# A two-layer hybrid trunk on one core: layer-norm sums on VectorE, five orders changed, and the last quarter of the first modulation cut in two

## The chip, the cores and the metric

The kernel runs on one core of a Trainium2 chip. Its engines are TensorE (PE; PEld is its weight load), VectorE (DVE), ScalarE (ACT), GpSimd (POOL) and SyncE (SP), which here only issues transfers. They run side by side and wait for each other through semaphores. The metric is the device time of one execution in microseconds (us); smaller is better.

## The reference, cut to what matters

Two layers act on x, 256 tokens of 2048 channels. All is float32.

```
cond = silu(c)
for layer in range(2):
    shift, scale, gate = split(cond @ w_ada[layer] + b_ada[layer])      # 2048 x 6144: the modulation
    h = rms_norm(x, norm_g) * (1 + scale) + shift
    qkv_a, z_a, ..., glu_in, z_b, q_c, k_c, v_c, z_c, ..., gate_raw = split(h @ w_in[layer])
    y_a = rms_norm(gated_delta_rule(...)) * silu(z_a)                   # branch a
    u   = causal_conv(a_half * sigmoid(b_half)) + conv_b_b
    y_b = silu(layer_norm(u)) * silu(z_b)                               # branch b: the layer norm over 1024 channels
    y_c = sparse_attention(...) * silu(z_c)                             # branch c
    merged = sum over a, b, c of sigmoid(gate_raw) * (y @ w_proj)
    x = x + gate * (merged @ w_out)
```

## The kernel before, in words

Activations lie channel by token: a tile `[128, KT, 256]` holds 16 blocks of 128 channels (`kt`), all 256 tokens in a row. Weights come in chunks of 256 rows by 512 columns (512 KB, two `kt`). A chunk passes four hands: SP loads it into one of four `raw` buffers (L377, after `w_split` says that the chunk four before it has been split), ACT rounds it into `wh` (L540, `rounds`, after PE has used the chunk four before it), POOL makes the rest `wl = raw - wh` (L519), and PE multiplies it (L908 to L910: three products for high and low halves). There are 672 chunks, 336 a layer. ACT's written order runs four chunks ahead of PE's. Every engine follows its own order written out by hand, so an instruction that waits holds up all that stands behind it on its engine. SP has one queue for all loads.

The stretches that the change touches, in order of time:

- **The first modulation** (layer 0). `cond @ w_ada` for shift and scale is done by DVE, in four quarters of 512 columns: `ada_part` (L1400 on) makes 16 multiply-adds of 128x1024 a quarter (512 columns of shift and of scale), from four `adaw` buffers that `ada_load` (L348) fills with 1 MB each, two `kt` at a time. The first three `kt` of the next quarter are done before `h_low` of this one. PE sums over partitions (`ada_sum(q)`, L988 to L991), DVE finishes the modulation (`quarter_mods`) and four blocks of h, ACT rounds them (`h_high`, L583), DVE makes the low half (`h_low`, L1477), and PE then runs its part of three pairs of PSUM banks over these four blocks (`part_gemm`, 144 products in six chunks). ACT's loop for quarter q is: round four chunks, `h_high(q)`, round two. After the fourth quarter a fourth pair follows over all 16 blocks.
- **The four turns of branch c** (`prep_turn`, L1737 on). While PE runs gate and projection products, DVE and PE work an inversion in levels; `between` is a hook of DVE behind levels 1 and 2. Turn 0 uses it.
- **The z groups.** 32 chunks, with the four steps of the scan between them. `ln_sum` (L1240) sums u over 1024 channels by eight products of `ones` with the eight blocks of `ub`; `ln_var` (L1247) does the same with the squares in `lnt`. ACT copies y_b to `yh` (L846) when DVE has it ready (`yb_ready`, L1912), between two stretches of `rounds`.
- **The turns of branches b and a.** DVE also accumulates the next modulations (`mod_unit`, 128x2048 from 1 MB `modw` buffers, two of them, `mod_load`, L389). A load of unit u waits until unit u-2 is done. `first` says from which `kt` the accumulator is in PSUM (banks 4 to 7) and not in SBUF (`acc`).
- **The output groups.** `w_out` in four groups of eight chunks, with the units of layer 1's scale between; `SCALE_AT` says behind which chunk (group, chunk) SP issues which unit's load, `UNIT_W` how many units DVE does before each group's result. At the layer's end PE sums the squares of x, ACT takes the root (`root_mean`, L545), and DVE and ACT build h of layer 1.

Of the kernel before, what the change touches and what calls it, by code (L numbers as in the profile page):

```python
# [24 lines left out]
P = 128  # L25
# [109 lines left out]
def trunk(nc, xt, cvec, rel_bias, w_ada, w_in, w_pa, w_pb, w_pc, w_out, b_gate, params, consts, hot, out):  # L135
    ctx = ExitStack()
    with ctx:
# [103 lines left out]
        lnt = sb("lnt", 122, [CT, T])  # L241

# [49 lines left out]
        def merged_ps(q):  # L292
# [31 lines left out]
        INV_Y = [11, 14, 17, 20, 23]  # L324

# [14 lines left out]
        def _(sp):  # L340
# [5 lines left out]
            def ada_load(n):  # L346

                q, j = n // 8, n % 8  # L348
                if n >= 4:
                    sp.wait_ge(sem("ada_used"), n - 3)  # L350
                for part in (SHIFT, SCALE):
                    col = part * D + q * GW
                    sp.dma_start(adaw[j % 4][:, :, part], wa[0, :, 2 * j:2 * j + 2, col:col + GW]
                                 ).then_inc(ada_landed[j % 4], 16)
# [14 lines left out]
            for layer in range(DEPTH):  # L369
# [154 lines left out]
        def _(act):  # L524
# [52 lines left out]
            for layer in range(DEPTH):  # L577
                L1 = layer + 1
                hc = layer * HCL
                def h_high(q):  # L580

                    act.wait_ge(sem("h_ready"), q + 1)
                    A.copy(ah[:, 4 * q:4 * q + 4], merged[:, 4 * q:4 * q + 4]).then_inc(sem("hh_ready"), 1)  # L583

                def shifted_high(n):

                    act.wait_ge(sem("h_ready"), 8 * layer - 4 + n + 1)
# [4 lines left out]
                if layer == 0:  # L592
                    for q in range(4):
# [3 lines left out]
                        hc += 6  # L597
                    rounds(hc, RING)
# [26 lines left out]
                for n, dst in enumerate((qk[:, 0:4], qk[:, 4:8], None, qi[:])):  # L625
# [7 lines left out]
                    if n == 0:  # L633
                        act.wait_ge(sem("hT_ready"), 8 * layer + 4)
# [208 lines left out]
                rounds(hc + 8, 2)  # L843
# [3 lines left out]
                rounds(hc + 10, 6, 2)  # L847
# [54 lines left out]
        def _(pe):  # L902
# [82 lines left out]
            def ada_sum(q):  # L985

                pe.wait_ge(sem("ada_summed"), q + 1)
                for part in (SHIFT, SCALE):  # L988
                    for j in range(4 * q, 4 * q + 4):
# [13 lines left out]
            for layer in range(DEPTH):  # L1003
# [10 lines left out]
                if layer == 0:  # L1014
# [3 lines left out]
                    for q in range(4):  # L1018
                        ada_sum(q)
                        pe.wait_ge(sem("hT_ready"), q + 1)  # L1020
                        for pair in range(3):
                            part_gemm(hc, pair, H, 4 * q, 4, G_IN)
                            hc += 2
# [3 lines left out]
                else:  # L1027
                    group(0, H, quarter=("hT_ready", 4 * layer, 1))
# [211 lines left out]
                def ln_sum():  # L1240
                    pe.wait_ge(sem("inv_u"), 6 * 4 * L1)
                    pe.wait_ge(sem("prep_wT"), 4 * L1 + 1)
                    for kt in range(CT):
                        mm = M.matmul(pb[3][:, 0:T], ones, ub[:, kt], start=kt == 0, stop=kt == CT - 1)
                    mm.then_inc(sem("ln_sum"), 1)

                def ln_var():  # L1247
                    pe.wait_ge(sem("ln_sq"), L1)
                    for kt in range(CT):
                        mm = M.matmul(pb[3][:, T:2 * T], ones, lnt[:, kt], start=kt == 0, stop=kt == CT - 1)  # L1250
                    mm.then_inc(sem("ln_var"), 1)
# [110 lines left out]
        def _(dve):  # L1362
# [29 lines left out]
            def normed_quarter(q):  # L1392

                V.tensor_tensor(merged[:, 4 * q:4 * q + 4], xs[:, 4 * q:4 * q + 4],
                                spread(rst[:], 1, [P, 4, T]), ALU.mult)

            def ada_part(q, k0, k1):

                wide, side = ps[:, 6:8, :], acc[:, :, q * GW:(q + 1) * GW]
                V.drain()  # L1400
                for kt in range(k0, k1):
                    j, m = kt // 2, kt % 2
                    if m == 0:
                        dve.wait_ge(ada_landed[j % 4], 32 * ((8 * q + j) // 4 + 1))
                    w = adaw[j % 4][:, m]
                    ahead = ADA_SIDE if q else 0
# [6 lines left out]
                    if m:  # L1413
# [624 lines left out]
```

## Time and profile before

| | us |
|---|---|
| median of 3 runs | 2340.78 (2339.74 to 2343.28) |
| the profiled execution | 2340.51 |
| its span, first to last instruction | 2338.7 |
| PE busy | 2255.2 (96%) |
| POOL busy | 1646.5 (70%) |
| DVE busy | 1141.1 (49%) |
| ACT busy | 955.9 (41%) |

A row of a timeline gives start and length of a run of like instructions, the engine, the line, what is written and read, and in brackets how long the engine had been idle and who ended that. A row of waits gives total, number of times and the longest. "The granted clock" is the share of full speed that TensorE had.

### The profile page before, as it was taken

To read this page: it belongs to the slowest core of one execution; us is meant where nothing else is said; L and a number is where in the kernel's file an instruction comes from. 1 tells how busy PE (TensorE), PEld (TensorE's weight loads), DVE (VectorE), ACT (ScalarE), POOL (GpSimd) and SP (SyncE) were. 2 spreads that over 40 slices of the span, in tenths; PEclk is the share of its full clock that TensorE was granted. 3 is DMA by queue.
4 is the path that set the end of the run, shared out by engine and by line. 5 is a ranking of instruction groups with operands and counts; after the bars stand their busy time and mean duration, and the time that the engine had idled before them with its cause. 6 is when DMAs were issued, how large, how long until landed. Compare 5 with 4: busy or idle time off the path is not lost.

```text
span 2338.7 us, 40293 instructions
## 1 busy us (share of the span) xinstructions
PE 2255.2 (96%) x16408; PEld 2040.3 (87%) x16408; DVE 1141.1 (49%) x1682; ACT 955.9 (41%) x1037; POOL 1646.5 (70%) x676
## 2 busy tenths in 40 slices
PE   5799999999999999999899999999999999999999
PEld 3789999987779988888899999998777899888899
DVE  5849883854443443443522894665544335421110
ACT  3234444472322544434234344437433244444442
POOL 1468778765554788987666886876655458888876
PEclk8789999999999999999999999999999999999999
DMA  9967545544442589897865664554444337976664
GB/s 370 386 210 225 164 142 177 161 148 124 129 137 92 200 310 332 296 329 284 323 208 181 195 213 142 168 166 145 138 134 134 113 118 279 343 233 190 204 207 154
DMA packets 228840, 479.65 MB, mean 205 GB/s; under 512 B 22080, under 2 KB 26304, under 8 KB 220128
## 3 DMA queue, kind: packets, MB, share of 16 engines
q1 hardware_dynamic: 227392, 475.50, 61.1%
q8 instruction: 99, 1.62, 0.3%
q10 hardware_dynamic: 1312, 2.23, 0.3%
q14 instruction: 37, 0.30, 0.0%
HBM read 471.25 MB, written 6.29 MB: 204 GB/s over the span
## 4 chain that ended last, share of the span: by engine, by line
POOL 48%; issue 35%; PE 16%; POOLq 1%; DVE 0%; ACT 0%; DVEq 0%; ACTq 0%
POOL wl L519 48%; PE ps L908 5%; PE ps L910 5%; PE ps L909 5%; POOLq L518 1%; PE ps L1331 0%; PE ps L997 0%; POOLq L514 0%; DVE xs L1985 0%; DVE ps L1709 0%; ACT gate L528 0%; POOLq L519 0%; DVEq L1367 0%; ACTq L770 0%; DVEq L1708 0%
## 5 line engine op out<-in xcount | busy, mean ns | idle before, releaser
L519 POOL TENSOR_TENSOR wl<-raw,wh 128x1024 fp32r<-128x1024 f32 x672 | 1646.3, 2460 | 679.2 <-ACT wh L540 677.8
L540 ACT CAST wh<-raw 128x1024 fp32r<-128x1024 f32 x672 | 702.8, 1049 | 1227.4 <-PE ps L910 1069.0
L908 PE MATMUL ps<-ah,wh 128*128 128x256 f32 x3008 | 873.8, 290 | 40.8 <-DVE al L1477 21.6
L909 PE MATMUL ps<-al,wh 128*128 128x256 f32 x3008 | 861.0, 286 | 0.0
L910 PE MATMUL ps<-ah,wl 128*128 128x256 f32 x3008 | 860.5, 286 | 0.0
L908 PEld LDWEIGHTS ps<-ah,wh 128*128 128x128 f32 x3008 | 588.0, 195 | 48.1 <-DVE al L1477 21.9
L909 PEld LDWEIGHTS ps<-al,wh 128*128 128x128 f32 x3008 | 587.8, 195 | 4.5 <-issue 4.1
L910 PEld LDWEIGHTS ps<-ah,wl 128*128 128x128 f32 x3008 | 587.4, 195 | 0.0
L908 PE MATMUL ps<-wh,ah 128*128 128x512 f32 (+1 forms) x832 | 325.7, 391 | 0.0
L910 PE MATMUL ps<-wh,al 128*128 128x512 f32 (+1 forms) x832 | 318.7, 383 | 0.0
L909 PE MATMUL ps<-wl,ah 128*128 128x512 f32 (+1 forms) x832 | 318.5, 383 | 0.0
L1543 DVE SCALAR_TENSOR_TENSOR ps<-upad,par,ps 128x256 f32<-128x256 f32 x480 | 199.7, 484 | 9.3 <-issue 0.4
L908 PEld LDWEIGHTS ps<-wh,ah 128*128 128x128 f32 x832 | 157.3, 189 | 31.2
L910 PEld LDWEIGHTS ps<-wh,al 128*128 128x128 f32 x832 | 157.0, 189 | 31.0
L909 PEld LDWEIGHTS ps<-wl,ah 128*128 128x128 f32 x832 | 157.4, 189 | 28.3
L1430 DVE SCALAR_TENSOR_TENSOR ps<-modw,cond,ps 128x2048 f32<-128x2048 f32 x50 | 117.8, 2356 | 111.0 <-DMA modw<-w_ada 107.4
L908 PE MATMUL ps<-wh,yh 128*128 128x512 f32 x384 | 155.5, 405 | 0.0
L909 PE MATMUL ps<-wl,yh 128*128 128x512 f32 x384 | 150.0, 391 | 0.0
L910 PE MATMUL ps<-wh,yl 128*128 128x512 f32 x384 | 149.8, 390 | 0.0
L1709 DVE TENSOR_TENSOR ps<-ps,gbias 128x1024 f32<-128x1024 f32 x24 | 29.5, 1230 | 138.5 <-PE ps L910 138.5
L908 PEld LDWEIGHTS ps<-wh,yh 128*128 128x128 f32 x384 | 72.0, 188 | 16.1 <-POOL wl L519 0.2
L910 PEld LDWEIGHTS ps<-wh,yl 128*128 128x128 f32 x384 | 72.1, 188 | 15.5
(259 smaller groups left out, 1810.9 us busy)
## 6 DMA issues: line engine op xcount, KB each, us to landing
raw<-w_in SPq DMA_DIRECT2D x512, 512.0 KB, 3.5
modw<-w_ada SPq DMA_DIRECT2D x64, 1024.0 KB, 7.6
adaw<-w_ada SPq DMA_DIRECT2D x64, 512.0 KB, 9.6
raw<-w_out SPq DMA_DIRECT2D x64, 512.0 KB, 5.0
raw<-w_pc SPq DMA_DIRECT2D x32, 512.0 KB, 3.6
raw<-w_pb SPq DMA_DIRECT2D x32, 512.0 KB, 5.7
raw<-w_pa SPq DMA_DIRECT2D x32, 512.0 KB, 4.9
gbias<-b_gate SPq DMA_DIRECT2D x24, 256.0 KB, 4.3
```

Source lines behind the costliest of these rows:

```text
L518: pool.wait_ge(sem("w_rounded"), i * SPLITS + (n + 1))
L519: nc.gpsimd.tensor_tensor(wl[:, s], raw[:, s], wh[:, s].bitcast(F32), ALU.subtract).then_inc(sem("w_split"), 1)
L540: A.copy(wh[:, s], raw[:, s]).then_inc(sem("w_rounded"), 1)
L908: M.matmul(o, lh, rh, start=start, stop=False, skip_group_check=True)
L909: M.matmul(o, lh, rr, start=False, stop=False, skip_group_check=True)
L910: return M.matmul(o, ll, rh, start=False, stop=last, skip_group_check=True)
L1430: unit = V.scalar_tensor_tensor(o, w, cond[:, kt:kt + 1], wide if first < kt <= last else side, ALU.mult, ALU.add)
L1543: V.scalar_tensor_tensor(o, upad[:, ct, back:back + T], w, o, ALU.mult, ALU.add)
L1709: V.tensor_tensor(ps[:, 0:2, :], ps[:, 0:2, :], spread(gbias[:], 1, [P, TT, GW]), ALU.add).then_inc(sem("gate_sum"), 1)
```

## The change

1. *Last quarter in two.* `PIECES` makes five pieces of the first modulation: three of 512 columns, two of 256. A load for a half piece brings four `kt` of 256 columns (1 MB as before). DVE does 16 multiply-adds of 128x512 for each half; of the last piece only `kt` 0 is done ahead. PE's `ada_sum(3)` stands between pair 1 and pair 2 of the third piece. SP's chunks of the last quarter come in the order of the halves. ACT's loop keeps its order, with `h_high(4)` behind it.
2. *Layer-norm sums.* DVE adds up the eight blocks (`tensor_reduce` over a view with 256 elements from one value to the next), for the sum in the hook of turn 2, for the squares behind `scan_v(2)`; PE makes one product of each.
3. *yh.* Three more chunks are rounded ahead of the copy to `yh`.
4. *Output groups.* `UNIT_S` 2 to 3, unit 2 of the last turn moves ahead of `merged_low(0)`; groups 0 to 3 do 2, 5, 5, 0 units in place of 4, 4, 4, 0; loads are placed anew.
5. *Root.* A one-column Sqrt on ACT behind the last three chunks, ahead of the squares.

```diff
-        UNIT_A, UNIT_W, UNIT_S = 4, 4, 2
+        UNIT_A, UNIT_S = 4, 3
+        UNIT_W = (UNIT_A, 6, 11, KT)
-        SCALE_AT = {(0, 3): 4, (0, 5): 5, (0, 6): 6, (0, 7): 7, (1, 1): 8, (1, 3): 9, (1, 5): 10, (1, 7): 11,
-                    (2, 1): 12, (2, 3): 13, (2, 5): 14, (2, 7): 15}
+        SCALE_AT = {(0, 4): 4, (0, 7): 5, (1, 1): 6, (1, 3): 7, (1, 4): 8, (1, 6): 9, (1, 7): 10,
+                    (2, 1): 11, (2, 3): 12, (2, 4): 13, (2, 6): 14, (2, 7): 15}
...
+        PIECES = ((0, GW), (GW, GW), (2 * GW, GW), (3 * GW, GW // 2), (3 * GW + GW // 2, GW // 2))
+        FIRST = len(PIECES)
...
-                    chunks = [(col, j) for q in range(4) for col in (first, second, first + GW)
-                              for j in range(2 * q, 2 * q + 2)]
+                    chunks = [(col, j) for q in range(3) for col in cols for j in range(2 * q, 2 * q + 2)]
+                    chunks += [(col, j) for j in (6, 7) for col in cols]
...
                         rounds(hc, RING, hc % RING)
                         h_high(q)
                         rounds(hc + RING, 2, (hc + RING) % RING)
                         hc += 6
+                    h_high(4)
...
-                rounds(hc + 8, 2)
+                rounds(hc + 8, 5)
                 act.wait_ge(sem("yb_ready"), L1)
                 act.wait_ge(sem("w_used"), proj_end)
                 A.copy(yh[:], ub[:]).then_inc(sem("yh_ready"), 1)
-                rounds(hc + 10, 6, 2)
+                rounds(hc + 13, 3, 1)
...
                     rounds(hc, 3)
+                    A.activation(craw[:, 0:1], epsb[:, 0:1], ACT.Sqrt)
...
-                    for q in range(4):
-                        ada_sum(q)
+                    for q in range(FIRST):
+                        if q != 3:
+                            ada_sum(q)
                         pe.wait_ge(sem("hT_ready"), q + 1)
...
                         for pair in range(3):
-                            part_gemm(hc, pair, H, 4 * q, 4, G_IN)
-                            hc += 2
+                            if q == 2 and pair == 2:
+                                ada_sum(3)
+                            part_gemm(hc, pair, H, tiles.start, n, G_IN)
+                            hc += n // HK
...
-                    for kt in range(CT):
-                        mm = M.matmul(pb[3][:, 0:T], ones, ub[:, kt], start=kt == 0, stop=kt == CT - 1)
-                    mm.then_inc(sem("ln_sum"), 1)
+                    pe.wait_ge(sem("ln_tiles"), L1)
+                    M.matmul(pb[3][:, 0:T], ones, lss[:, 0], start=True, stop=True).then_inc(sem("ln_sum"), 1)
...
+                        ahead = ADA_SIDE if q < FIRST - 2 else 0
...
-                        ada_part(q, ADA_SIDE + 1 if q else 10, KT)
+                        ada_part(q, 10 if q == 0 else ADA_SIDE + 1 if q < FIRST - 1 else 1, KT)
-                        if q < 3:
-                            ada_part(q + 1, 0, ADA_SIDE)
+                        if q < FIRST - 1:
+                            ada_part(q + 1, 0, ahead)
                         quarter_mods(q)
...
-                        if q < 3:
-                            ada_part(q + 1, ADA_SIDE, ADA_SIDE + 1)
+                        if q < FIRST - 1:
+                            ada_part(q + 1, ahead, ahead + 1)
                         h_low(q)
...
+                def ln_tiles(n):
+
+                    if n == 0:
+                        V.tensor_reduce(lss[:, 0], ub[:].rearrange("p c t -> p t c"), AX.X, ALU.add
+                                        ).then_inc(sem("ln_tiles"), 1)
...
-                    prep_turn(i, split_yc if i == 0 else None)
+                    prep_turn(i, split_yc if i == 0 else ln_tiles if i == 2 else None)
...
                 scan_v(2)
+                V.drain()
+                V.tensor_reduce(lss[:, 1], lnt[:].rearrange("p c t -> p t c"), AX.X, ALU.add
+                                ).then_inc(sem("ln_sq"), 1)
                 z_silu(2, 0, zs[1])
...
+                units(2, 3)
                 for q in range(3):
                     merged_low(q)
                 merge(3, hc, 12 * layer + 8, False)
-                units(2, 4)
+                units(3, 4)
                 merged_low(3)
...
-                            for kt in range(UNIT_A + UNIT_W * j, UNIT_A + UNIT_W * (j + 1)):
+                            for kt in range(UNIT_W[j], UNIT_W[j + 1]):
```

## Rows read from the trace of the kernel before

**Rows 1.** The page's first line.
```profile
span 2338.7 us, 40293 instructions
```
**Rows 2.** Waits of PE, whole span: total us, times, longest.
```profile
PE ps L908 <- DVE al L1477: 21.6, 4, 6.4
PE ps L990 <- DVEq L1415: 17.4, 4, 13.4
PE ps L908 <- POOL wl L519: 12.9, 6, 3.8
PE ps L908 <- issue: 6.3, 1, 6.3
```
**Rows 3.** Timeline of PE, the third and fourth quarter.
```profile
115.31 0.58 PE L908 MATMUL ps<-ah,wh 128*128 128x256 f32 x1 [6.37 <-DVE al L1477]
...
136.72 2.13 PE L990 MATMUL ps<-con,acc 128*128 128x1 f32 x16 [1.27 <-DVEq L1415]
143.23 0.58 PE L908 MATMUL ps<-ah,wh 128*128 128x256 f32 x1 [4.39 <-DVE al L1477]
```
**Rows 4.** Timeline of DVE, the fourth quarter.
```profile
116.47 9.53 DVE L1411 SCALAR_TENSOR_TENSOR ps<-adaw,cond,ps 128x1024 f32<-128x1024 f32 x7
...
135.34 1.28 DVE L1411 SCALAR_TENSOR_TENSOR acc<-adaw,cond,ps 128x1024 f32<-128x1024 f32 x1
...
139.46 1.38 DVE L1501 TENSOR_SCALAR merged<-merged,gsc,mods 128x256 f32<-128x256 f32 x4
141.95 1.23 DVE L1477 TENSOR_TENSOR al<-merged,ah 128x1024 fp32r<-128x1024 f32 x1 [1.11 <-ACT ah L583]
```
**Rows 5.** Timeline of ACT, the end of the fourth quarter.
```profile
135.54 1.05 ACT L540 CAST wh<-raw 128x1024 fp32r<-128x1024 f32 x1 [1.83 <-PE ps L910]
140.87 1.04 ACT L583 CAST ah<-merged 128x1024 fp32r<-128x1024 f32 x1 [4.29 <-DVE merged L1501]
```
**Rows 6.** DVE's instructions by line and form: busy us, mean ns.
```profile
L1759 DVE TENSOR_TENSOR vb<-ps,hbeta 128x512 f32<-128x512 f32 x8 | 5.5, 693 | 0.2
```
**Rows 7.** Windows of 5 us: PE, PEld, DVE, ACT, POOL busy, granted clock, DMA share, GB/s.
```profile
825.00:830.00 5.00, 4.66 (x22) 4.66 (x23) 0.53 (x1) 0.00 (x0) 4.96 (x4) 0.50 0.75 269
...
1145.00:1150.00 5.00, 5.00 (x44) 5.00 (x43) 3.06 (x2) 2.09 (x2) 4.57 (x3) 1.00 1.04 405
```
**Rows 8.** Timeline of PE, the first layer-norm sum.
```profile
703.29 3.62 PE L1244 MATMUL ps<-ub,con 128*128 128x256 f32 x16
```
**Rows 9.** DVE's instructions by line and form: a reduction.
```profile
L1634 DVE TENSOR_REDUCE mx<-probs 128x8 f32<-128x2048 f32 x2 | 4.6, 2286 | 0.1
```
**Rows 10.** Timeline of DVE in turn 2 and behind the third step of the scan.
```profile
677.46 0.42 DVE L1789 TENSOR_TENSOR xm<-ps,con 128x256 f32<-128x256 f32 x1 [3.27 <-PE ps L1192]
...
743.08 1.22 DVE L1700 SCALAR_TENSOR_TENSOR zs<-zt,ps 128x1024 f32<-128x1024 f32 x1 [5.16 <-ACT zt L528]
```
**Rows 11.** Timeline of PE, the waits behind the copy to yh.
```profile
825.34 0.58 PE L908 MATMUL ps<-ah,wh 128*128 128x256 f32 x1 [3.43 <-POOL wl L519]
...
1964.42 0.57 PE L908 MATMUL ps<-ah,wh 128*128 128x256 f32 x1 [2.33 <-POOL wl L519]
```
**Rows 12.** Timeline of ACT, the first copy to yh.
```profile
818.85 1.90 ACT L846 CAST yh<-ub 128x2048 fp32r<-128x2048 f32 x1 [7.31 <-DVE ub L1912]
```
**Rows 13.** Waits of PE from 1100 to 1200 us.
```profile
PE ps L908 <- POOL wl L519: 6.8, 3, 3.8
```
**Rows 14.** Timeline of SP's queue, the first output group.
```profile
1087.14 11.59 SPq L377 DMA_DIRECT2D raw<-w_out  x4
1115.55 0.34 SPq L389 DMA_DIRECT2D modw<-w_ada  x1
```
**Rows 15.** Timeline of DVE, unit 2 of the scale.
```profile
1113.01 2.51 DVE L1430 SCALAR_TENSOR_TENSOR ps<-modw,cond,acc 128x2048 f32<-128x2048 f32 x1 [0.29 <-issue]
```
**Rows 16.** Timeline of ACT, the root at the layer's end.
```profile
1226.44 1.28 ACT L545 ACT_TABLE_LOAD   x1
```
**Rows 17.** Timeline of PE, the last sum of squares.
```profile
1224.76 1.99 PE L970 MATMUL ps<-merged,con 128*128 128x256 f32 x8 [1.63 <-ACT merged L895]
```

More of the change, by code:

```diff
@@ L988, in ada_sum @@
                 for part in (SHIFT, SCALE):
-                    for j in range(4 * q, 4 * q + 4):
+                    for j in range(piece_tiles(q).start, piece_tiles(q).stop):
                         mm = M.matmul(pb[2][:, part * KT + j:part * KT + j + 1], acc[:, part, j * P:(j + 1) * P],
@@ L1027, in _ @@
                 else:
-                    group(0, H, quarter=("hT_ready", 4 * layer, 1))
+                    group(0, H, quarter=("hT_ready", FIRST * layer, 1))
                     group(1, H)
@@ L1392, in normed_quarter @@
             def normed_quarter(q):
-                V.tensor_tensor(merged[:, 4 * q:4 * q + 4], xs[:, 4 * q:4 * q + 4],
-                                spread(rst[:], 1, [P, 4, T]), ALU.mult)
+                tiles = piece_tiles(q)
+                V.tensor_tensor(merged[:, tiles], xs[:, tiles],
+                                spread(rst[:], 1, [P, tiles.stop - tiles.start, T]), ALU.mult)
             def ada_part(q, k0, k1):
-                wide, side = ps[:, 6:8, :], acc[:, :, q * GW:(q + 1) * GW]
+                (first, per), (at, width) = piece_loads(q), PIECES[q]
+                wide, side = ps[:, 6:8, at % GW:at % GW + width], acc[:, :, at:at + width]
                 V.drain()
                 for kt in range(k0, k1):
-                    j, m = kt // 2, kt % 2
+                    j, m = first + kt // per, kt % per
                     if m == 0:
-                        dve.wait_ge(ada_landed[j % 4], 32 * ((8 * q + j) // 4 + 1))
-                    w = adaw[j % 4][:, m]
-                    ahead = ADA_SIDE if q else 0
+                        dve.wait_ge(ada_landed[j % 4], 32 * (j // 4 + 1))
+                    w = piece_weights(adaw[j % 4], q)[:, m]
+                    ahead = ADA_SIDE if 0 < q < 4 else 0
                     o = wide if ahead <= kt < KT - 1 else side
@@ L1453, in quarter_mods @@
             def quarter_mods(q):
[L1455 removed]
+                part = piece_tiles(q)
+                k0, n = part.start, part.stop - part.start
                 dve.wait_ge(sem("ada_turned"), q + 1)
[L1457 to L1460 removed]
+                for side in (SHIFT, SCALE):
+                    at = side * KT + k0
+                    last = V.tensor_tensor(mods[:, at:at + n], pb[2][:, at:at + n], p_(0, "b_ada", at, n), ALU.add)
+                if q == FIRST - 1:
                     last.then_inc(sem("mods_ready"), 1)
                 V.drain()
[L1463 to L1464 removed]
+                V.scalar_tensor_tensor(gsc[:, part], mods[:, KT + k0:KT + k0 + n], 1.0,
+                                       p_(0, "norm_g", k0, n), ALU.add, ALU.mult)
                 V.drain()
@@ L1487, in _ @@
                 if layer == 0:
-                    for q in range(4):
+                    for q in range(FIRST):
+                        ahead = ADA_SIDE if q < FIRST - 2 else 0
                         if q == 0:
@@ L1496, in _ @@
                             dve.wait_ge(sem("con_landed"), 16)
-                        if q < 3:
-                            ada_part(q + 1, 0, ADA_SIDE)
+                        if q < FIRST - 1:
+                            ada_part(q + 1, 0, ahead)
                         quarter_mods(q)
-                        for kt in range(4 * q, 4 * q + 4):
+                        for kt in range(piece_tiles(q).start, piece_tiles(q).stop):
                             m = V.tensor_scalar(merged[:, kt], merged[:, kt], gsc[:, kt:kt + 1], mods[:, kt:kt + 1],
```

51 lines of the change are left out of this document (30 added, 21 removed).

## The prediction

> **What bounds the kernel now.** I read the page first. The span is 2338.7 us [rows 1] and the execution took 2340.51, 1.81 outside the span; the median of the runs is 2340.78, so the sum below, made against 2340.51, stands for the median within 0.3. PE is busy in 96% of the span, POOL in 70%, DVE in 49%: PE sets the time, and a change is worth what it takes from PE's own work or from PE's waits. So the second view is the list of PE's waits [rows 2]. Four groups matter: 21.6 us before the products that need h of a quarter, 17.4 before the sums of the first modulation, 12.9 in six waits for POOL's halves, and one of 6.3 at the layer's end (named "issue"; the root's chain lies in it). The third view is each engine's timeline around them. A wait costs more than its length: behind the one of 3.43 [rows 11] the granted clock is 0.50, TensorE's lower level of 1.2 GHz, and a window of 5 us holds 22 products, where another at 1.00 holds 44 [rows 7]. About 26 products of 0.21 us run there instead of at 0.12, so I add 2.6 us to a wait of this length.
>
> **First modulation: +2.9.** Take it in the order of time. The units of the fourth quarter done ahead become half as wide. A unit of 1024 takes 1.36 from start to start (9.53 for 7) [rows 4]; a two-input instruction of 512 from PSUM takes 0.69 [rows 6], a multiply-add is 0.07 longer and the gap behind it 0.07, so 0.83. Two such units stand ahead of the third quarter's h, so PE starts that (third) quarter at 113.9 and not at 115.31 [rows 3]: -1.4. Its 144 products end 20.1 later as before (136.72 less 1.27 idle is 135.45 [rows 3]), and the sum for the first half, half of the 2.13 [rows 3], now stands between them: 135.1. DVE has its half long done (13 units of 0.83 behind h_low and the norm: 125.4), but waits for that sum until 129.3, since PE takes it only behind pair 1; nothing else stands ahead of DVE's wait, because no unit of the last half is done ahead of it. Then it makes two blocks of h by 130.7 and one unit of the last half.
>
> Here is the step that I think decides. ACT's order was not changed: it rounds four chunks and only then does h_high(3). The fourth of them, row 135.54, waits for PE's use of the last chunk of the third quarter [rows 5]. Before, that cost nothing, because h came at 140.87 [rows 5]; now h is ready at 130.7 and ACT sits in front of the rounding until 135.1. Rounding 1.05, h_high on half the elements 0.6, h_low half of 1.23 [rows 4]: PE gets the first half's h at 137.4, so it stands 2.3 us, and DVE stands too, from 131.6 to 136.8. Only then come the norm of two blocks (0.7) and 15 units of 0.83, 12.5: the last sum is ready at 150.6, where the whole quarter was ready at 136.6 before (135.34 + 1.28 [rows 4]). The loads do not bind: their last unit before ran at 135.34, and now none is read before 138. PE's 72 products for the first half (8.6) end at 146. Behind 150.6 come the sum (1.1), the modulation (0.6), two blocks (half of 1.38), h_high 0.6 and h_low 0.65 [rows 4, 5]: 154.6. The 72 products left take 8.6, and 2 more at the lower clock: 165.2. Before, PE started at 143.23 [rows 3] and 144 products took 17.3 and 2.3: 162.8. With 0.5 for the clock behind the earlier start: **+2.9**. Bounds: if DVE's short units run at 0.69 and the clock rises early, 2 us less and 1 more for it, so 0; if a short unit costs as much as half a long one plus a whole 0.3 of overhead (0.98), 15 of them add 2.3, and late loads of 1 KB rows 1 more: +6.
>
> **Layer-norm sums: -12.1.** A sum of eight products is 16 records in 3.62 with the tail of the last, 3.45 from start to start [rows 8]; two products' records of 16 stay, so 14 x 0.216 = 3.0 go. There are four (two a layer): -12.1. PE is full there, so the whole is path, if DVE's reductions are covered. A reduction of 2048 contiguous values takes 2.29 [rows 9]. In turn 2 DVE idles 3.27 before the row 677.46 [rows 10]; the reduction stands in that gap, and PE reads the next `xm` 1.5 later, so 4.2 are free. Behind scan_v(2) DVE idles 5.16 before 743.08 [rows 10]. `ln_var` is asked for some 11 us behind scan_v(2). At 2.29 both are hidden. No row shows the strided view: bounds 2.29 and four times that, 9.2; I take 2.3 to 4.2, cost 0. At 9.2 the first delays PE by 5 a layer.
>
> The Trainium skill (Advanced Engine Details and Errata, section Memory Cachelines) speaks against this: reads that hit a different 16-byte line each time pay a penalty, and here each value is 1 KB from the next. It names no size. By the page the reduction is longer than row 9's; by the sum nothing is owed until it passes 4.2. It is a rival below.
>
> **yh: -6.0 and -3.9.** ACT waits 7.31 for y_b [rows 12] and copies for 1.90, and the chunk behind reaches PE late: 3.43 and 2.33 of wait [rows 11]. With three more chunks rounded first, these are ready in time (PE uses one in 2.88, and they are asked for from 822 on); the copy runs from 820.1 and not 818.85, between two roundings. Behind it, chunk 13 of the row is rounded 1 late, with 6 to spare; DVE's low half of y is 1.3 later, and PE asks for it over 20 us later. SP's next unit loads wait for units behind that low half: a mod load moves to 827 from 830, so it keeps ahead of PE, which gains 6. Layer 0: 3.43 + 2.6 = -6.0. Layer 1: 2.33 and a shorter stretch of low clock, 1.6: -3.9. Bounds: nothing lost, or half given back to loads: -5 to -10.
>
> **Output groups: -9.0.** SP stands between 1098.7 (1087.14 + 11.59) and 1115.55 [rows 14], because the load behind chunk (0,3) waits for unit 2, which DVE does at 1113.01 [rows 15], behind a merge. The `w_out` chunks queued behind it come late, and PE waits 6.8 in three waits [rows 13], the first of 3.8 [rows 2], with the 2.6 of clock behind it. With unit 2 done before merged_low(0), at 1096 to 1100, in ACT's shadow, and the load one chunk later, chunk (0,4) is issued at 1103.4. The waits go: -9.4. What is late next: SP stands at (1,4) for unit 6, which DVE does behind group 0's result (PE ends that group at 1133.6, result 1.7, unit 2.4: 1137.9). The unit's load and chunk (1,5) behind it then land by 1144.2, rounding 1.05 and POOL 2.4 end at 1147.6, and PE comes to this chunk at 1148.0. Groups 1 and 2 hold 5 loads of 1.05 MB and 8 chunks of 0.52, 9.4 MB: at the 405 GB/s of a full window [rows 7] 23.3 us against PE's 23.0, so it stays that close, chunk after chunk, through both; I take 0.4 of wait. **-9.0**, bounds -4 (each of groups 1 and 2 loses 2.5) and -10.
>
> **Root: -0.9.** ACT loads its table from 1226.44 for 1.28 [rows 16] while PE's last sum of squares ends at 1226.75 (1224.76 + 1.99) [rows 17]. The load now falls in ACT's idle time before the squares. The root can start at 1226.8 and not 1227.7: -0.9, within the 6.3 wait [rows 2]. Bounds 0 and -1.3.
>
> **Sum.** +2.9 - 12.1 - 6.0 - 3.9 - 9.0 - 0.9 = -29.0. 2340.5 - 29.0 = 2311.5, which stands for the median.
>
> **Rivals.**
> - *The half pays.* ACT and DVE pass the first half sooner than I think, and the start of the layer gains: the term is 0 or below (-3 at the end). For it: DVE idles 5 us in this stretch by my sum. Against: row 135.54. Time 2306 to 2308.5. Chance 0.15.
> - *The loads bind the output groups.* SP's waits at (1,4) and (2,4) come late enough to empty the queue, and half of the 9.0 is given back. Time 2316. For it: 23.3 against 23.0. Chance 0.15.
> - *The strided reduction is slow.* At 9.2 us it delays the inversion in turn 2 by 5 a layer: 2321.5. Chance 0.07. This is the rule of the page above.
> - *Slower than before.* The same mechanism further on: in turn 2, PE waits for every us beyond 4.2; behind scan_v(2) for every us beyond about 11. The gain of 29.0 is used up when a layer loses 14.5, that is at a reduction of about 15 us (10.8 + 4), 7.3 ns a value against 1.1 in row 9's. Then the time is 2341 and above that slower. Nothing in the rows is so slow. Chance 0.02.
> - *The change does not do what it says.* The waits behind yh stay, because POOL and not ACT holds the chunks (its halves take 2.4, PE's chunk 2.88). Then 10 are missing: 2321. Chance 0.04.
>
> **Numbers.** The forecast has 0.57, with its own range 2308 to 2315. To reach 8 in 10 and to take in the bounds (start 0 to +6, output -4 to -10, yh -5 to -10) the range goes from 2304 to 2319. A change of 0.2% (4.7 us) is about what can be told here. Faster: 0.96; within: 0.02; slower: 0.02.
>
> **What would show it.** PE's wait for the first half's h at about 135 to 137.5, ended by ACT's order (h_high(3) behind the rounding of chunk 21), and its first product of the last half near 154.6. Lines of the layer-norm sums with 2 records each and no wait. No wait for POOL behind yh; at most 1 us of it between 1100 and 1200. One table load less in front of the root. DVE's reductions at 2.3 to 4.2. The forecast is wrong if the start of the fourth pair is not 2 to 4 later than before, if a reduction passes 4.2, or if waits for POOL in the output groups pass 2 us.

## The result, and the profile after

The changed kernel takes 2320.89 us (2320.60 to 2321.02, 4 runs) where the kernel before took 2340.26 beside it (2338.14 to 2343.28, 4 runs): ratio 0.9916, 95% interval 0.9902 to 0.9930. It is 19.4 us faster; 29.0 were forecast. The profiled execution took 2320.99 with a span of 2319.2, against 2340.51 and 2338.7 [rows 1], so the two traces differ by 19.5 and can be laid side by side. One execution of a kernel below, the one with the layer-norm sums alone, took 2804.78 at a granted clock of 0.73 and is left out of its median.

First, where PE waits. The view of PE's waits in the changed kernel (engine, what and line waited for, total us, times, longest), which answers to [rows 2]:

```profile
PE ps L931 <- DVE al L1506: 29.1, 5, 8.1
PE ps L1013 <- DVEq L1442: 17.6, 2, 15.7
PE ps L931 <- POOL wl L539: 5.3, 10, 0.8
PE ps L931 <- issue: 5.3, 1, 5.3
```

POOL's waits fell from 12.9 in six to 5.3, but in ten: the long ones went and small ones came. The waits for h rose from 21.6 in four to 29.1 in five.

Second, in which stretch the time went. All 672 weight chunks come in the same order on PE in both kernels, except the last six of the first modulation, so I took the time at which PE ends each chunk, and compared the length of the stretches between such times. Layers and their parts are those of the text on the kernel before; differences to the kernel before, in us; chunks that are not listed moved by 0.0:

| stretch (chunks) | forecast | measured |
|---|---|---|
| first modulation (to 23) | +2.9 | +6.4 |
| from there to the z groups (to 175) | 0 | -1.9 |
| layer-norm sums, layers 0 and 1 (176-187, 512-523) | -12.1 | -6.05, -6.05 |
| chunks behind the copy to yh (206-207, 542-543) | -6.0, -3.9 | -6.3, -4.1 |
| the turns behind them (208-255, 544-591) | 0 | +3.5, +1.1 |
| output groups 0 and early 1 (304-316) | -9.4 | -10.1 |
| the rest of the output groups (317-335) | +0.4 | +3.4 |
| root and first chunks of layer 1 (336-339) | -0.9 | -0.4 |
| all others (256-303, 340-511, 592-end) | 0 | -1.6, +0.9, +1.6 |
| sum | -29.0 | -19.5 |

*The start.* PE, then ACT, then DVE in the changed kernel (start and length in us, engine, line, what, count, idle before and who ended it); the PE rows answer to [rows 3], the others to [rows 4, 5]:

```profile
141.33 0.58 PE L931 MATMUL ps<-ah,wh 128*128 128x256 f32 x1 [5.93 <-DVE al L1506]
154.47 1.05 PE L1013 MATMUL ps<-con,acc 128*128 128x1 f32 x8 [1.98 <-DVEq L1442]
158.29 0.58 PE L931 MATMUL ps<-ah,wh 128*128 128x256 f32 x1 [2.77 <-DVE al L1506]
...
137.27 1.04 ACT L560 CAST wh<-raw 128x1024 fp32r<-128x1024 f32 x1 [3.30 <-DMA raw<-w_in]
138.22 0.61 ACT L604 CAST ah<-merged 128x512 fp32r<-128x512 f32 x1
...
130.13 2.72 DVE L1531 TENSOR_SCALAR merged<-merged,gsc,mods 128x256 f32<-128x256 f32 x2
...
138.87 2.41 DVE L1506 TENSOR_TENSOR al<-merged,ah 128x512 fp32r<-128x512 f32 x1 [5.16 <-ACT ah L604]
...
141.96 11.59 DVE L1438 SCALAR_TENSOR_TENSOR ps<-adaw,cond,ps 128x512 f32<-128x512 f32 x14
```

The order is the one forecast: h's two blocks are ready at 132.85 (130.13 + 2.72), yet ACT rounds them at 138.22, right behind a rounding of weights. That rounding waited for its load and not, as I wrote, for PE alone: it began at 137.27, where I had it begin at 135.1. PE got the first half's h at 141.33 (forecast 137.4) and the last half's at 158.29 (forecast 154.6). The 14 units of 0.83 are as forecast (11.59 for 14).

Why that load was late is in SP's queue and in one window of each trace, the first two rows from the changed kernel, the last from the kernel before (columns of the windows as in [rows 7]):

```profile
127.66 25.95 SPq L396 DMA_DIRECT2D raw<-w_in  x7
106.00:137.00 31.00, 22.29 (x170) 21.80 (x169) 21.06 (x32) 7.34 (x7) 15.29 (x7) 0.83 1.09 361
```
```profile
106.00:136.00 30.00, 22.65 (x160) 22.36 (x160) 24.65 (x26) 6.96 (x8) 14.22 (x6) 0.77 1.04 380
```

SP issued the load at 127.66, about as before (127.58), and it landed at 137.25, where before it landed at 135.22. The transfer engines are full in both kernels (shares 1.09 and 1.04), but they move 361 GB/s and not 380: two thirds of the bytes now come in rows of 1 KB (the half pieces), and such a row takes 51 ns where one of 2 KB takes 89. The load was close to binding before, too: it landed 0.32 ahead of the rounding at 135.54 [rows 5].

POOL's rows of the same stretch say why a pair of DVE instructions that takes 0.73 at 156.12 took 2.72, and one that takes 0.69 at 157.54 took 2.41:

```profile
129.98 2.40 POOL L539 TENSOR_TENSOR wl<-raw,wh 128x1024 fp32r<-128x1024 f32 x1 [0.49 <-ACT wh L560]
134.05 2.38 POOL L539 TENSOR_TENSOR wl<-raw,wh 128x1024 fp32r<-128x1024 f32 x1 [1.67 <-ACT wh L560]
138.39 2.34 POOL L539 TENSOR_TENSOR wl<-raw,wh 128x1024 fp32r<-128x1024 f32 x1 [1.97 <-ACT wh L560]
```

Each of the two DVE rows begins inside a POOL half and ends some 0.5 behind it: 132.85 against 132.38, 141.28 against 140.73. DVE seems to have stood until POOL was nearly through. The Trainium skill (SBUF — State Buffer, section Who interferes with whom) has this as an exclusive lock between DVE and GpSimd, taken by DVE's instructions with two SBUF inputs and by some with one; both rows fit it.

*Layer-norm sums.* DVE's reductions by line and form (busy us, mean ns); contiguous values took 2286 [rows 9]. Behind them PE's first sum:

```profile
L1923 DVE TENSOR_REDUCE lss<-lnt 128x256 f32<-128x2048 f32 x2 | 7.8, 3882 | 0.2
L1856 DVE TENSOR_REDUCE lss<-ub 128x256 f32<-128x2048 f32 x2 | 7.7, 3825 | 0.0
...
707.79 0.60 PE L1272 MATMUL ps<-lss,con 128*128 128x256 f32 x2
```

The strided view costs 1.7 times the contiguous one. This agrees with the rule on 16-byte lines in the Trainium skill (Advanced Engine Details and Errata, section Memory Cachelines), which names no size; here it is 3.9 us and not 9, under the 4.2 from which it would cost. PE's part fell from 3.62 [rows 8] to 0.60 with 2 records.

*yh.* DVE and then POOL in the changed kernel, behind the first copy to yh:

```profile
813.01 4.33 DVE L1951 SCALAR_TENSOR_TENSOR ub<-ub,zs 128x2048 f32<-128x2048 f32 x1
820.46 3.67 DVE L1953 TENSOR_TENSOR yl<-ub,yh 128x2048 fp32r<-128x2048 f32 x1 [3.12 <-ACT yh L868]
...
810.74 27.15 POOL L539 TENSOR_TENSOR wl<-raw,wh 128x1024 fp32r<-128x1024 f32 x8
```

POOL makes eight halves without a pause and takes 3.39 each, over PE's 2.88 a chunk. Then PE waits 0.33, 0.68 and 0.78 for it at 826, 836 and 853, and again at 957. The two long waits of [rows 11] are gone.

*Output groups.* SP's queue, then windows of 10 us in the changed kernel (PE, PEld, DVE, ACT, POOL busy, granted clock, DMA share, GB/s):

```profile
1122.73 0.37 SPq L396 DMA_DIRECT2D raw<-w_out  x1
1131.99 0.34 SPq L408 DMA_DIRECT2D modw<-w_ada  x1
...
1130.00:1140.00 10.00, 10.00 (x86) 10.00 (x85) 6.68 (x3) 2.10 (x2) 3.90 (x3) 1.00 0.70 240
1140.00:1150.00 10.00, 9.36 (x76) 8.95 (x75) 4.67 (x2) 3.05 (x3) 7.06 (x3) 1.00 1.03 411
```

The first output group no longer waits. SP's stand for unit 6 is there as forecast, and it lasts 9 us (1123.1 to 1131.99). The load ahead of it landed at 1129.76, so the queue was empty for over 2 us (DMA share 0.00 from 1130 to 1132, 0.70 until 1140), and then full at 411 GB/s while PE runs short.

*Root.* The table load is out of the chain (ACT loads it at 1208.83, PE's sums of squares start at 1212.18), and PE's wait "issue" is 5.30 where it was 6.26 (the 6.3 of [rows 2]). It is 5.30 or 5.31 in every kernel below with the early Sqrt, and 6.25 in the three without.

### The profile page after: what moved, and what is told of

Read it like the earlier page. It is cut to its first block, busy times and chain, and to the rows that moved or that the text cites. A ratio compares the mean times of both kernels' runs of the same rounds, so it can differ in the third digit from the quotient of the medians.

```text
span 2319.2 us, 40232 instructions
## 1 busy us (share of the span) xinstructions
PE 2236.6 (96%) x16352; PEld 2022.0 (87%) x16352; DVE 1174.9 (51%) x1707; ACT 956.2 (41%) x1039; POOL 1655.5 (71%) x676
## 4 chain that ended last, share of the span: by engine, by line
POOL 48%; issue 35%; PE 15%; POOLq 1%; DMA 0%; DVE 0%; ACT 0%; DVEq 0%; ACTq 0%
POOL wl L539 48%; PE ps L931 5%; PE ps L933 5%; PE ps L932 5%; POOLq L538 1%; PE ps L1356 0%; DMA raw<-w_in 0%; PE ps L1020 0%; POOLq L534 0%; DVE xs L2025 0%; DVE ps L1739 0%; ACT wh L560 0%; ACT gate L548 0%; POOLq L539 0%; DVEq L1392 0%
## 5 line engine op out<-in xcount | busy, mean ns | idle before, releaser
L931 PE MATMUL ps<-ah,wh 128*128 128x256 f32 x3008 | 871.9, 290 | 36.6 <-DVE al L1506 29.1
```

The source lines that it names most:

```text
L931: M.matmul(o, lh, rh, start=start, stop=False, skip_group_check=True)
```

## The experiments

Each kernel ran with the kernel before on the same chip. Single executions there mostly lie within 4 us of their median, a few 7 or 8 off, the kernel before too (2335.66 to 2349.85 in all), and move with the granted clock (0.981 to 0.974). So differences of 2 or 3 us between two kernels are read from the stretches and not from the medians. The differences to the kernel before, in the stretches of the table above:

| kernel | start | to 175 | sums, both | yh, both | turns, both | out 304-316 | out 317-335 |
|---|---|---|---|---|---|---|---|
| changed, first profile | 6.4 | -1.9 | -12.1 | -10.4 | 3.5, 1.1 | -10.1 | 3.4 |
| changed, again | 6.6 | -3.4 | -12.1 | -10.4 | 1.6, 1.2 | -10.1 | 3.9 |
| no halves | 0.1 | 0.0 | -12.1 | -10.4 | 2.6, 1.3 | -10.1 | 3.8 |
| h rounded earlier | 1.0 | -1.8 | -12.1 | -10.4 | 0.6, 1.7 | -10.1 | 3.6 |
| groups 4, 4, 4 | 6.1 | -1.9 | -12.1 | -10.4 | 1.1, 1.2 | -10.1 | -1.6 |
| one SBUF input | 6.5 | -3.3 | -12.1 | -10.4 | -0.1, 0.0 | -10.1 | 3.6 |
| narrow gate loads | 6.9 | -3.3 | -12.1 | -10.4 | 1.4, 1.7 | -10.1 | 4.9 |
| three repairs | -1.3 | -3.3 | -12.1 | -10.4 | 2.3, 1.1 | -10.1 | 0.0 |
| no halves, groups 4, 4, 4 | 0.7 | 0.1 | -12.1 | -10.4 | 1.7, 1.5 | -10.1 | -1.6 |
| sums alone | 0.1 | 0.1 | -12.1 | -0.5 | 1.0, 0.0 | 2.8 | -1.6 |
| yh alone | 0.3 | 0.0 | 0.0 | -10.4 | 1.1, 0.7 | -0.1 | 0.0 |
| output alone | 0.9 | 0.0 | 0.0 | -3.1 | -0.1, 0.3 | -10.1 | 4.5 |

**The changed kernel with the first modulation as before (no halves).** All other parts of the change stay.

```
-        PIECES = ((0, GW), (GW, GW), (2 * GW, GW), (3 * GW, GW // 2), (3 * GW + GW // 2, GW // 2))
...
+                    for q in range(4):
+                        ada_sum(q)
```

> The changed kernel with the first modulation as before (four quarters); layer-norm sums, yh, output groups and root stay as changed. Theory (the halves cost what the two traces show: the fourth pair of the first stage starts 6.4 us later, because ACT's order holds h_high(3) behind the rounding of chunk 21 and DVE then has 15 short units left): 2320.9 - 6.4 = 2314.5, and PE's first product of the last quarter starts near 143 again. Rival (the halves gain and what is missing lies elsewhere): above 2321. Rival (they cost only the 2.9 us that I forecast): 2318.

Measured: 2315.99 (2308.66 to 2317.33), ratio 0.9883 (0.9864 to 0.9902). The start falls back to +0.1. The halves cost 6.3 in the start. Of that, 1.8 to 3.4 comes back before chunk 175 in every kernel with halves, and nothing in those without: the low clock near 290 is shorter or absent there (last section).

**h of the first half rounded earlier.** ACT rounds two chunks and not four before it.

```
-                        rounds(hc, RING, hc % RING)
+                        early = 2 if q == 3 else RING
+                        rounds(hc, early, hc % RING)
                         h_high(q)
-                        rounds(hc + RING, 2, (hc + RING) % RING)
+                        rounds(hc + early, 6 - early, (hc + early) % RING)
```

> The changed kernel with one order changed on ACT: in the last quarter it rounds two chunks, then does h_high(3), then rounds four (before: four, h_high(3), two). Theory (ACT's order is the cause): h_high(3) runs near 133 instead of 138.2, PE starts the first half near 135.5 instead of 141.3, DVE starts its 15 units 5 us earlier, and the time falls by 4 to 5.5 us to about 2316. Rival (the short units and the loads, not ACT's order, are the cost): PE's wait moves to the second half and the time stays within 1 us of 2320.9.

Measured: 2315.48 (2311.8 to 2320.2), ratio 0.9894 (0.9878 to 0.9910). Its PE, ACT and DVE rows:

```profile
148.54 1.87 PE L1014 MATMUL ps<-con,acc 128*128 128x1 f32 x8 [3.61 <-DVEq L1443]
153.18 0.58 PE L932 MATMUL ps<-ah,wh 128*128 128x256 f32 x1 [2.77 <-DVE al L1507]
...
133.78 0.62 ACT L604 CAST ah<-merged 128x512 fp32r<-128x512 f32 x1 [2.99 <-DVE merged L1532]
...
134.67 0.69 DVE L1507 TENSOR_TENSOR al<-merged,ah 128x512 fp32r<-128x512 f32 x1
```

ACT now takes h the moment DVE has it (133.78), DVE's low half finds POOL idle and takes 0.69, and PE has no wait of the first half left. The last half's h comes at 153.18 and not at 158.29, and the start falls by 5.4, to +1.0. So ACT's order is the cause of that much, as the prediction's "step that decides" says.

**Output units in groups of 4, 4, 4, 4.** Each group does four units, so the unit that waits for a group's result comes later in the queue.

```
-        UNIT_W = (UNIT_A, 6, 11, KT)
+        UNIT_W = (UNIT_A, 8, 12, KT)
-        SCALE_AT = {(0, 4): 4, (0, 7): 5, (1, 1): 6, (1, 3): 7, (1, 4): 8, (1, 6): 9, (1, 7): 10,
-                    (2, 1): 11, (2, 3): 12, (2, 4): 13, (2, 6): 14, (2, 7): 15}
+        SCALE_AT = {(0, 4): 4, (0, 7): 5, (1, 1): 6, (1, 2): 7, (1, 4): 8, (1, 6): 9, (1, 7): 10,
+                    (2, 1): 11, (2, 2): 12, (2, 4): 13, (2, 5): 14, (2, 7): 15}
```

> The changed kernel with groups 0 to 2 of the output doing 4, 4, 4 units (in place of 2, 5, 5) and the loads placed to match. Theory (SP stands until 1132 for unit 6, which waits for group 0's result, so the queue runs dry and the loads then bind: 3.4 us given back): unit 6 runs near 1123, the load behind (1,4) is issued near 1125 instead of 1132, and 2.5 to 3.4 us come back: about 2318. Rival (9.4 MB a group against 23.0 us of PE bind by themselves, wherever the loads stand): within 1 us of 2320.9.

Measured: 2317.46 (2313.09 to 2318.77), ratio 0.9899 (0.9884 to 0.9913). SP's queue and the two windows in this kernel:

```profile
1123.88 0.34 SPq L408 DMA_DIRECT2D modw<-w_ada  x1
1124.31 3.23 SPq L396 DMA_DIRECT2D raw<-w_out  x2
...
1130.00:1140.00 10.00, 10.00 (x86) 10.00 (x85) 4.75 (x3) 3.58 (x4) 9.08 (x5) 1.00 1.02 388
1140.00:1150.00 10.00, 10.00 (x85) 10.00 (x84) 5.22 (x4) 3.15 (x3) 8.20 (x4) 1.00 1.02 391
```

The load behind chunk 3 of the group goes out at 1123.88 and not at 1131.99, the transfer engines are full from 1130 on, and no wait of PE for POOL stands between 1100 and 1200. The stretch falls from +3.4 to -1.6. Of these 5.0, the queue is 3.4: the other 1.6 is clock, a low stretch behind the sums of the scale that stands at 1200 in the kernel before and at 1188 in the changed one and is missing here. The same bytes pass: an empty queue is what cost, not the rate.

**The changed kernel again,** on the chip of the next three.

> The changed kernel once more, as it stands, so that the kernels beside it have it on their own chip. No theory differs on it: 2321 by its first runs, and of the stretches of its matmul row the layer-norm ones and the output ones as before; turns of branch b of layer 0 give back between 0.6 (as with the third rounding moved) and 3.5 us, if the amount depends on which low-clock windows and loads an execution gets.

Measured: 2321.95 (2321.09 to 2328.88), ratio 0.9915 (0.9896 to 0.9934), as at first. The turns of layer 0 give back 1.6 here and gave back 3.5 in the first profile: the amount is a matter of the execution. PE's waits for POOL there are 0.85 in place of 2.37, and DVE's four large two-input instructions beside them took 12.8 in place of 15.4.

**One SBUF input.** The four DVE instructions of 128x2048 with two SBUF inputs around the copy to yh become instructions of one input. Left out: the products with the norm's gate and with zs, and the true low half of y_b.

```
-                V.scalar_tensor_tensor(ub[:], ub[:], 0.25, zs[1][:], ALU.mult, ALU.mult).then_inc(sem("yb_ready"), 1)
+                V.tensor_scalar(ub[:], ub[:], 0.25, None, ALU.mult).then_inc(sem("yb_ready"), 1)
...
-                V.tensor_tensor(yl[:], ub[:], yh[:].bitcast(F32), ALU.subtract).then_inc(sem("y_split"), 1)
+                V.tensor_scalar(yl[:], ub[:], 0.001, None, ALU.mult).then_inc(sem("y_split"), 1)
```

> Leaves out the product with the norm's gate, the product with zs and the true low half of y_b and y_a: the four VectorE operations of two SBUF inputs over 128x2048 that stand between the gating units become operations of one SBUF input. Theory (GpSimd's weight halves are slow beside VectorE operations of two SBUF inputs, and that is what gives back 3.5 of the 6.3 us in layer 0): the GpSimd halves there stay near 2.4 us instead of 4.4, VectorE's four operations fall from 15.4 to under 10 us together, and the turns of branch b of layer 0 give back 0.5 us or less (-3), layer 1's 0.3 (-0.8): 2317. Rival (GpSimd runs back to back there since its order was caught up by TensorE, whatever VectorE does, or the loads come late by themselves): give-back stays at 2.5 or more, within 1 us of the changed kernel.

Measured: 2315.10 (2312.62 to 2315.35), ratio 0.9878 (0.9859 to 0.9897); 6.9 below the changed kernel beside it, more than the 4 expected. POOL in this kernel, the same stretch:

```profile
811.91 13.93 POOL L539 TENSOR_TENSOR wl<-raw,wh 128x1024 fp32r<-128x1024 f32 x5
826.04 2.41 POOL L539 TENSOR_TENSOR wl<-raw,wh 128x1024 fp32r<-128x1024 f32 x1 [0.19 <-ACT wh L560]
828.73 7.84 POOL L539 TENSOR_TENSOR wl<-raw,wh 128x1024 fp32r<-128x1024 f32 x3 [0.29 <-ACT wh L560]
```

Nine halves take 24.2, 2.69 each, where eight took 27.15, and POOL waits for ACT again instead of being behind. DVE's four instructions took 8.9 together. Nothing is given back in either layer (-0.1, 0.0), where the changed kernel beside it gave back 1.6 and 1.2. That is 2.9; another 3.1 is clock, in stretches no edit touches (256-303 and 592 on). This bears out the theory and excludes the rival that POOL falls behind whatever DVE does. The edit took an input away and made the instructions shorter at once, so it can't tell these two apart.

**Narrow gate loads.** Units 2 to 15 of layer 0's gate bring an eighth of their columns, so their results are not the gate's. An earlier form, which narrowed units 0 and 1 too, gave no result; in it I had still held the loads for the cause.

```
+                    wide = D // 8 if l == 0 and part == GATING and kt > 1 else D
```

> Loads an eighth of the columns for units 2 to 15 of layer 0's gate projection (the rest of each tile is stale data; the multiply-adds have the same sizes), so that some 12 MB less are loaded in and after the turns of layer 0's input projection. Theory (the weight halves on GpSimd are late, not the loads): the give-back in the turns of branch b falls by at most 1.5 us of the 3.5, since only what hangs on late loads goes. Rival (the transfer queues are what the gained time runs into): give-back falls to 0.5 or less, 3 us faster than the changed kernel, and the DMA share of the window falls below 0.8 with no wait of GpSimd on raw left.

Measured: 2321.95 (2319.07 to 2326.06), ratio 0.9909 (0.9891 to 0.9927): nothing. Windows of 814 to 834 in the changed kernel, and then in this one:

```profile
814.00:834.00 20.00, 19.67 (x135) 18.19 (x134) 16.44 (x7) 9.09 (x9) 19.96 (x7) 1.00 0.81 299
```
```profile
814.00:834.00 20.00, 19.76 (x130) 17.77 (x128) 14.18 (x7) 9.90 (x9) 19.96 (x7) 1.00 0.68 203
```

The DMA share falls from 0.81 to 0.68 and POOL stays at 19.96 of 20; the turns give back 1.4. In layer 0, the loads are not what the gained time ran into.

**Three repairs in one.** h rounded earlier, groups of 4, 4, 4, 4, and three of the last half's units done in `acc` ahead of its turn.

```
-                    ahead = ADA_SIDE if 0 < q < 4 else 0
+                    ahead = 0 if q == 0 else ADA_SIDE if q < 4 else 3
...
-                        ada_part(q, 10 if q == 0 else ADA_SIDE + 1 if q < FIRST - 1 else 1, KT)
+                        ada_part(q, 10 if q == 0 else ADA_SIDE + 1 if q < FIRST - 1 else 4, KT)
...
+                        if q == 3:
+                            ahead = 3
```

> The changed kernel with three edits: the rounding of h's first half ahead of all but two weight roundings, three units of the last half's multiply-adds ahead of its turn (acc in SBUF), and the output units in groups of 4, 4, 4, 4. Theory: ACT's order costs 5.3 us at the start, the halves' units after the first half 2.5 us more, the gap of the output groups 5.0 us: start +6.4 becomes -1 to -2, output +3.4 becomes -1.6; 2321 - 12.8 = 2308, and 2306 to 2311 by the clock. Rival (the start's loss is the low clock that follows any stop of that length, and it comes back at another place; the loads of the output matrix are what binds at 1140): 2313 or more.

Measured: 2307.00 (2304.64 to 2311.85), ratio 0.9848 (0.9827 to 0.9869), the best of all and as expected (2308). PE's rows and one of DVE's:

```profile
135.94 0.38 PE L932 MATMUL ps<-ah,wh 128*128 128x256 f32 x1 [1.06 <-DVE al L1507]
146.57 1.05 PE L1014 MATMUL ps<-con,acc 128*128 128x1 f32 x8 [1.75 <-DVEq L1443]
150.39 0.58 PE L932 MATMUL ps<-ah,wh 128*128 128x256 f32 x1 [2.77 <-DVE al L1507]
...
129.32 3.56 DVE L1439 SCALAR_TENSOR_TENSOR acc<-adaw,cond,acc 128x512 f32<-128x512 f32 x2
```

The last half's h is at 150.39, 2.8 before that of the second experiment: three units of 0.83 are 2.5. In `acc`, in SBUF, two units take 3.56 beside POOL's half and not 1.6, but in time that was idle. The output's rest came to 0.0 and not to the -1.6 of the run with groups alone; the low-clock stretch falls into it here (at 1173), as in the kernel before, so 3.4 is what the groups are worth.

**The layer-norm sums alone, the copy to yh alone, the output units alone,** each put into the kernel before.

> The kernel before with the layer-norm sums alone changed. Theory (eight matmuls fewer in each of four sums, VectorE's two reductions hidden): -6.05 us in each layer's layer-norm stretch and nothing given back, 2341 - 12.1 = 2329, give or take 1.6 for the low clock. Rival (the 3.85 us reductions take VectorE time that the turns of branch b or a later stage wants back): 2332 or more, with a positive difference in the stretch behind.

> The kernel before with the places of the high half of y_b alone changed. Theory (6.3 and 4.1 us saved by TensorE move its demand for weights forward, and GpSimd, whose halves are slow beside VectorE's operations of two SBUF inputs, can't follow): -6.3 and -4.1, of which 1.1 to 3.5 and 0.8 to 1.7 are given back in the turns of branch b, 2341 - 7 = 2334. Rival (the give-back belongs to all of the time gained since the start, the layer-norm sums above all, not to this edit): give-back under 0.8 in layer 0, 2331.

> The kernel before with the output units alone changed (4, 2, 5, 5 and the places of the scales). Theory (the unit of group 1 whose tile waits for group 0's result holds the load queue back, whatever came before): -10.1 at outputs 0 and 1, +3.4 to +3.9 behind them, 2341 - 6.5 = 2334.5. Rival (the give-back comes of the time gained earlier, which leaves the queue less far ahead): -10.1 and at most +1.5, 2332.

Measured, beside 2340.14 of the kernel before: sums 2329.8 (2326.40 to 2336.48, 6 runs), ratio 0.9954 (0.9937 to 0.9970); yh 2334.22 (2330.75 to 2339.11), 0.9973 (0.9965 to 0.9982); output 2338.75 (2332.42 to 2344.77), 0.9992 (0.9981 to 1.0004). The first two are as expected, the third is 4 above. For its stretches, the first was run once more:

> The kernel with the layer-norm sums alone changed once more, for its stretches, since the first profile of it was taken at a granted clock of 0.73 throughout. Theory (the layer-norm sums save 6.05 us in each layer whatever stands behind, and give back what GpSimd can't follow only together with the high half of y_b): -6.05 and -6.05 with under 0.5 given back in the turns of branch b. Rival (each microsecond gained before the turns of branch b is partly given back there): 0.5 to 2 given back in layer 0.

The sums are exact in it, -6.05 in each layer. What follows them is not clear: +1.0 stands in layer 0's turns, 0.76 of it one wait for POOL at 955.48, as the rival has it, and 0.0 in layer 1's, as the theory has it. And the -1.2 right before, at chunks 206 and 207, is mostly clock: the wait for POOL there is 3.29 where it was 3.43, with less of the low clock behind it. One execution does not decide between the sides. yh alone gives -6.3 and -4.1 and gives back 1.1 and 0.7: the give-back needs nothing but this edit, and more of it comes with the other parts. The output alone gives -10.1 and +4.5, over the expected 3.4 to 3.9, so its give-back is its own. Here, too, the low-clock stretch of the kernel before at 1200 is missing, which hides 1.6: the queue cost some 6.1, with 5.1 of waits for POOL. The -3.1 at the chunks behind yh is the wait there, followed by less of the low clock in this execution. Yet its median is only 1.4 lower (0.9981 to 1.0004), where the two output stretches make 5.6. The profiled execution took 2334.46 and the others up to 2344.77; by which of them this part should be priced alone stays open.

**No halves, groups of 4, 4, 4, 4.**

> The changed kernel with the first modulation as before and the output units in groups of 4, 4, 4, 4. Theory: the run without halves gave 2316 and the gap of the output groups costs 3.4 to 5.0, so 2311 to 2313; beside the version with halves and units ahead (2307.0, its start 1.4 us shorter than before) this says whether the halves are worth their code: 1.5 us or more slower than that one. Rival (halving brings nothing even with its two repairs): within 1 us of it, 2306 to 2308.

Measured: 2315.16 (2310.64 to 2318.46, 4 runs; 2311 to 2313 were expected), ratio 0.9896 (0.9880 to 0.9913), against 0.9848 with halves and repairs. The rival (within 1 us) is out: with their two repairs the halves gain. The profiles have 2.0 of that in the start. Another 3.4 up to chunk 175 is the low clock near 290, which is there in this kernel and absent in the other; whether the halves or chance keep it away is not shown. The rest, some 3 us of the medians, is not placed.

## Why the prediction was wrong

The direction held, and the three large gains came at their own places; the time was missed by 9.5 us and fell outside the range (2304 to 2319), and the miss has four terms.

1. **First modulation, +2.9 forecast, +6.4 measured: 3.5 of the miss.** The step that I called deciding, ACT in front of a rounding with h ready, is right, and took 5.4 us by experiment. Mis-sized is its end. "ACT sits in front of the rounding until 135.1" took PE's use of the buffer for the last condition and left out the load of that chunk, which landed at 137.25 behind loads in rows of 1 KB and held ACT until 137.27; and h_low was priced at half of 1.23 while it ran into POOL's half (2.41). 2.2 and 1.8 are, to 0.1, the 3.9 by which PE's 141.33 is later than 137.4, and all that follows is about as late (158.29 for 154.6). "The loads do not bind" was asked of the `adaw` buffers, not of `raw`; the "late loads of 1 KB rows" stood only among the bounds, at 1 us. The rival that the half pays fell for this kernel, and holds with the repairs. The clock fell behind both stops of PE (0.50 from 140 to 145, 0.67 from 155 to 160), where I had it behind the second alone; the first cost nothing, since PE had its 72 products done 2 us before the next sum was ready.

2. **yh, -9.9 forecast, -10.4 measured at the place, but 3.5 and 1.1 given back: 4.2 of the miss in the net.** The prediction had POOL's half at 2.4 throughout, and PE's chunk at 2.88, "with 6 to spare". In this stretch DVE runs its large two-input instructions, and POOL takes 3.4 a half. The bound "half given back to loads" had the size right and the cause wrong: loads cost nothing (narrow loads), DVE's large two-input instructions all of it (one SBUF input).

3. **Output groups, -9.0 forecast, -6.7 measured: 2.3.** The -9.4 of the waits was right (10.1). "23.3 against 23.0, so it stays that close, chunk after chunk" is the step that failed. It supposed a queue that is always full. SP stood for 9 us and the queue ran empty, and at a full rate there is nothing to catch up with; 3.4 was lost, not 0.4. My rival that loads bind there, with half of the 9.0 given back, was nearer. It was an edit of the order that undid it, with the same bytes.

4. **Root, -0.9 forecast, -0.4 here: 0.5.** The wait itself fell by 0.96 (6.26 to 5.30), as forecast. The stretch as a whole lies between -0.4 and -1.1 in kernels with the edit, and between +0.1 and -0.5 in those without, so the 0.5 is not the root's. The stretches that no edit touches gave 1.0 back, by the clock.

The layer-norm term was exact, -12.1, and the doubt about the strided view was settled at 3.9. One thing in its working was wrong without effect: I put the first reduction before the row 677.46 [rows 10]; that row is of turn 3. The reduction runs at 628.77, behind level 1 of turn 2, which has the same pattern of gaps, and delays the next `xm` by 0.4. The slower rival and the one that POOL holds the chunks behind yh did not occur.

## What to carry to other kernels

When an engine's written order puts an urgent short step behind a routine one, price the routine one by all that it waits for, the load too, and move the urgent step ahead of it: this alone was 5.4 us. Where a transfer queue is near its full rate, a stand of the queue can't be made up later; place loads so that the one whose buffer comes free last is last, even if each unit then runs later. And price GpSimd's step beside what VectorE does at the time: a half that takes 2.4 alone took 3.4 beside large two-input VectorE work, which turned POOL from ample to late.

## What the runs showed of the hardware that I had not expected

- DVE and POOL hold each other up instruction by instruction: DVE work of 0.73 took 2.72 and ended 0.5 behind POOL's half. DVE's reduction is free of it: the row of 3.88 at 739.48 runs beside a POOL half of 2.40, each at its usual length.
- Summing eight blocks at a stride of 1 KB took 3.83 to 3.88 against 2.29 for contiguous values, the same in five kernels.
- The granted clock has stretches of 0.50, the lower level of 1.2 GHz, not only behind stops of PE. Behind 32 sums of one column, in which PE counts as busy for 3.6 us, it often falls too: in the changed kernel at 297, 1085, 1188, 1416 (while the sums still run) and 2085. It doesn't always: behind those that end at 964 it stays at 1.00. Here is PE in the kernel before, and then in the one with three repairs, at such a place (the pair behind the sums is the same work):

```profile
285.52 4.28 PE L1060 MATMUL ps<-con,sqk 128*128 128x1 f32 x32
289.66 2.05 PE L1062 MATMUL ps<-sqk,con 128*128 128x512 f32 x2
```
```profile
284.04 3.66 PE L1089 MATMUL ps<-con,sqk 128*128 128x1 f32 x32
287.56 1.10 PE L1091 MATMUL ps<-sqk,con 128*128 128x512 f32 x2
```

  Which of them get it shifts with small changes of timing ahead. Each costs 1.6 to 3.4 us, which is the size of the jumps in the stretches that no edit touches, and of much of the spread between executions of one program (up to 11 us on one chip here). I took the low clock for a price of waits alone.
